# Moving the lower splits of the down chunks from VectorE to GpSimd

## The chip, the cores and the metric

The kernel runs on one core of one Trainium2 chip. The metric is the device time of one execution in microseconds (us). Before the change the median of three runs is 1020.29 us (1019.63 to 1021.06). For this kernel about 0.2% (2 us) is what a measurement can tell from no change.

## The reference

The reference is two transformer-like blocks over 256 tokens of width 1024, in float32. The first block mixes a gated spatial branch and a gated causal convolution and ends in a feed-forward of width 4096. The second block has two layers: differential attention and a gated feed-forward, then latent attention (called here the second attention) and a second gated feed-forward. The change touches these parts:

```python
def conv_ffn(h, w_up, conv_w, conv_b, w_down):      # FFN_HIDDEN = 2816, both layers
    u = h @ w_up                                    # 256 x 1024 @ 1024 x 5632
    c = causal depthwise convolution of width 3 over u, + conv_b
    g, val = jnp.split(c, 2, axis=-1)
    return (jax.nn.silu(g) * val) @ w_down          # 256 x 2816 @ 2816 x 1024

def mla_attention(h, w_in, ..., w_uq, w_ukv, w_o, cos, sin):
    proj = h @ w_in
    q = (rms_norm(proj[..., :384]) @ w_uq) ...      # 16 heads of 64 + 32
    kv = (rms_norm(proj[..., 384:640]) @ w_ukv) ...
    ... masked softmax per head ...
    return o @ w_o
```

Each layer adds the result to x and normalises x before the next.

## The kernel before

**Precision by splitting.** Every weight matrix is read once, in chunks. A chunk lands in SBUF as float32 in one of the raw slots (`raw`, or `q_sb` where that buffer is free), 128 partitions by up to 2048 words. ScalarE copies it, rounded, into the upper half of a ring slot (`whl[..., 0, ...]`, L1267): the upper split. VectorE then writes raw minus upper into the lower half (`whl[..., 1, ...]`, L1763): the lower split. TensorE multiplies upper by upper, upper by lower and lower by upper (L623 to L625, L630 to L632, L825 and L827). So each chunk passes DMA, ScalarE, VectorE and TensorE, in the order of its number n. `hi_ready` and `lo_ready` count the upper and lower splits, `chunk_used` the chunks that TensorE has finished. The ring has four slots: ScalarE may split chunk n once TensorE has used n - 4. The DMA queue (SyncE) loads into a raw slot once the lower split of the chunk that was in it is counted.

**A gated feed-forward** has 22 units (`FB`), one for each 128 hidden columns of the gate and of the value. Unit j has an up chunk (128 x 2048 words, the two halves of `w_up`) and a down chunk (128 x 1024 words, one block of rows of `w_down`). TensorE's order is up j+3, down j+1, and so on, in turn: it runs two ups ahead of the downs. The chunks are numbered in that order within the stage (`n0 + m`): m = 0, 1, 2, 4, 6, ..., 38, 39 are up chunks, m = 3, 5, 7, ..., 37, 40, 41, 42, 43 are down chunks (`is_down`). The last up (39) stands ahead of the last four downs.

Unit j on VectorE, in program order (function `unit` within `ffn`): take the up sum out of PSUM and scale it by the reciprocal deviation (`conv_in`); lower split of the next down chunk, `split(0)`; four convolution taps (L2043, `conv_out`); the product of silu(gate) and value (`t_dve`, L2054); lower split of an up chunk, `split(1)`; and the rest of the rounded product (`lat`, L2058). ScalarE in the same unit: the convolution's first tap with the bias (L1439, after `conv_in`), an upper split of an up chunk, silu (L1444), the rounded product (L1452), an upper split of a down chunk. In the first gated feed-forward the sum is read and scaled in one instruction (L2032, PSUM times `rstd`). In the second (`WIDE`) TensorE makes two sums, ScalarE copies the second (L1431, `t_act`), VectorE adds them (L2028) and scales in place (L2030, `conv_in` times `rstd`).

**At the ends.** Behind the last unit of the first gated feed-forward VectorE splits the first two chunks of the second attention (N_MLA, N_MLA + 1), and only then adds the sums into xT (L2090) and makes the tiles hT (L1838) that TensorE waits for. In the second attention, eight steps of two heads each, VectorE also splits the chunks of `w_uq` (768 words) and of `w_o` (N_WO2 and the three behind it, 2048 words each).

**GpSimd** only copies the rotated key to 16 heads (L1745), once. The program's order on each engine is written out by hand; nothing is scheduled.

## Time and profile before

| | |
|---|---|
| median of three runs | 1020.29 us |
| the profiled execution's own time | 1021.66 us |
| its span, first to last instruction | 1019.8 us |
| TensorE busy | 1003.1 us (98%) |
| VectorE busy | 760.3 us (75%) |
| ScalarE busy | 573.4 us (56%) |
| GpSimd busy | 6.6 us (1%) |
| mean granted TensorE clock | 0.999 of full speed |

Rows of the trace name an engine (PE is TensorE, DVE VectorE, ACT ScalarE, POOL GpSimd), a line of the kernel, out<-in by the program's names, and the partitions by elements. In brackets stands how long the engine had been idle before the row, and what it had waited for. The stages lie thus in the span: differential attention from 427 us, first gated feed-forward from about 536 to 722 us, second attention to 826 us, second gated feed-forward from 826 us to the end.

### The profile page before, as it was taken

How to read it: one execution, taken by the hardware profiler on the slowest of the kernel's cores; microseconds unless marked ns; L12 is line 12 of the kernel's file. 1: busy time of each engine (PE TensorE's matmuls, PEld its weight loads, DVE VectorE, ACT ScalarE, POOL GpSimd, SP SyncE). 2: the span in 40 equal slices, each digit the busy share in tenths (PEclk: the TensorE clock that was granted, in tenths of full speed). 3: DMA queues.
4: the chain of work that ended last, by engine and by line, in shares of the span. 5: the costliest groups of instructions: out<-in, count | busy, mean ns of one | idle time of the engine just before them, and what ended most of it. 6: DMA issues, size and time to landing. Idle time of an engine off the chain costs nothing.

```text
span 1019.8 us, 18671 instructions
## 1 busy us (share of the span) xinstructions
PE 1003.1 (98%) x7220; PEld 932.5 (91%) x7220; DVE 760.3 (75%) x1017; ACT 573.4 (56%) x820; POOL 6.6 (1%) x20
## 2 busy tenths in 40 slices
PE   7999999999999999999999999999999999999997
PEld 6999999999999999977899999999998898888886
DVE  7576655557766656787778877778877888888886
ACT  6543454445544445657866555555646675666665
POOL 0000000000000000000000000000020000000000
PEclk9999999999999999999999999999999999999999
DMA  8645566556665564354464666674324574766651
GB/s 300 211 147 184 184 204 199 171 165 200 199 206 180 191 205 181 128 204 128 167 198 124 189 185 185 186 211 143 125 63 104 166 223 136 216 191 192 191 158 76
DMA packets 191265, 178.87 MB, mean 175 GB/s; under 512 B 17444, under 2 KB 169586, under 8 KB 191218
## 3 DMA queue, kind: packets, MB, share of 16 engines
q1 hardware_dynamic: 191074, 177.96, 56.5%
q8 instruction: 32, 0.52, 0.2%
q10 hardware_dynamic: 144, 0.26, 0.1%
q14 instruction: 15, 0.12, 0.0%
HBM read 177.15 MB, written 1.05 MB: 175 GB/s over the span
## 4 chain that ended last, share of the span: by engine, by line
PE 88%; DVE 5%; ACT 3%; DMA 2%; issue 1%; SPq 0%; DVEq 0%; ACTq 0%
PE psum L623 17%; PE psum L625 17%; PE psum L624 17%; PE psum L825 13%; PE psum L827 7%; PE psum L630 4%; PE psum L632 4%; PE psum L631 4%; DVE whl L1763 2%; ACT whl L1267 1%; DMA raw<-da_w_qkv 1%; DMA raw<-mla_w_o 1%; PE psum L973 1%; PE psum L957 1%; DMA x_rows<-x 1%
## 5 line engine op out<-in xcount | busy, mean ns | idle before, releaser
L1763 DVE TENSOR_TENSOR whl<-raw,whl 128x2048 fp32r<-128x2048 f32 (+2 forms) x145 | 298.2, 2061 | 79.0 <-ACT whl L1267 78.4
L1267 ACT ACTIVATE whl<-raw 128x2048 fp32r<-128x2048 f32 (+2 forms) x145 | 248.3, 1716 | 77.5 <-DMA raw<-w_ff 29.1
L623 PE MATMUL psum<-hT,whl 128*128 128x256 f32 (+1 forms) x784 | 219.9, 280 | 1.0 <-DVE hT L1838 1.0
L624 PE MATMUL psum<-hT,whl 128*128 128x256 f32 (+1 forms) x784 | 218.9, 279 | 0.0
L625 PE MATMUL psum<-hT,whl 128*128 128x256 f32 (+1 forms) x784 | 218.9, 279 | 0.0
L825 PE MATMUL psum<-hT,whl 128*128 128x512 f32 x608 | 213.0, 391 | 0.1
L827 PE MATMUL psum<-hT,whl 128*128 128x256 f32 x608 | 171.4, 282 | 0.0
L623 PEld LDWEIGHTS psum<-hT,whl 128*128 128x128 f32 (+1 forms) x784 | 147.1, 188 | 1.5 <-issue 0.7
L624 PEld LDWEIGHTS psum<-hT,whl 128*128 128x128 f32 (+1 forms) x784 | 147.2, 188 | 0.1
L625 PEld LDWEIGHTS psum<-hT,whl 128*128 128x128 f32 (+1 forms) x784 | 147.1, 188 | 0.0
L623 PE MATMUL psum<-lat,whl 128*128 128x256 f32 (+1 forms) x512 | 144.1, 281 | 0.3 <-DVE whl L1763 0.3
L624 PE MATMUL psum<-lat,whl 128*128 128x256 f32 (+1 forms) x512 | 142.9, 279 | 0.0
L625 PE MATMUL psum<-lat,whl 128*128 128x256 f32 (+1 forms) x512 | 142.9, 279 | 0.0
L825 PEld LDWEIGHTS psum<-hT,whl 128*128 128x128 f32 x608 | 114.1, 188 | 24.4 <-DVE whl L1763 0.5
L827 PEld LDWEIGHTS psum<-hT,whl 128*128 128x128 f32 x608 | 114.9, 189 | 0.8
L1439 ACT ACTIVATE conv_out<-conv_in,vcol 128x256 f32<-128x256 f32 x88 | 48.2, 595 | 92.7 <-DVE conv_in L2032 55.8
L623 PEld LDWEIGHTS psum<-lat,whl 128*128 128x128 f32 (+1 forms) x512 | 95.4, 186 | 2.6 <-issue 1.1
L624 PEld LDWEIGHTS psum<-lat,whl 128*128 128x128 f32 (+1 forms) x512 | 95.4, 186 | 0.1
L625 PEld LDWEIGHTS psum<-lat,whl 128*128 128x128 f32 (+1 forms) x512 | 95.4, 186 | 0.0
L2043 DVE SCALAR_TENSOR_TENSOR conv_out<-conv_in,vcol,conv_out 128x256 f32<-128x256 f32 x176 | 73.6, 479 | 8.8 <-ACT conv_out L1439 8.1
L1763 DVE TENSOR_TENSOR whl<-q_sb,whl 128x2048 fp32r<-128x2048 f32 (+1 forms) x44 | 77.0, 1750 | 0.5 <-ACT whl L1267 0.5
L1267 ACT ACTIVATE whl<-q_sb 128x2048 fp32r<-128x2048 f32 (+1 forms) x44 | 64.9, 1475 | 1.1 <-PE psum L625 1.1
(258 smaller groups left out, 1583.0 us busy)
## 6 DMA issues: line engine op xcount, KB each, us to landing
raw<-w_ff SPq DMA_DIRECT2D x32, 1024.0 KB, 5.6
raw<-w_in SPq DMA_DIRECT2D x24, 1024.0 KB, 5.1
raw<-ffn_w_up SPq DMA_DIRECT2D x44, 512.0 KB, 5.1
q_sb<-ffn_w_up SPq DMA_DIRECT2D x44, 512.0 KB, 5.1
raw<-da_w_qkv SPq DMA_DIRECT2D x12, 1024.0 KB, 5.2
q_sb<-ffn_w_down SPq DMA_DIRECT2D x22, 512.0 KB, 3.8
raw<-ffn_w_down SPq DMA_DIRECT2D x22, 512.0 KB, 3.8
raw<-w_proj_a SPq DMA_DIRECT2D x4, 1024.0 KB, 5.2
```

The lines of the kernel that those rows point to most:

```text
L623: mm(dst, weight(n, 0, cols, kt, c0, m), hi, start=start, stop=False, skip_group_check=True)
L624: mm(dst, weight(n, 0, cols, kt, c0, m), lo, start=False, stop=False, skip_group_check=True)
L625: return mm(dst, weight(n, 1, cols, kt, c0, m), hi, start=False, stop=stop, skip_group_check=True)
L630: mm(dst, hi, w_hi, start=start, stop=False, skip_group_check=True)
L631: mm(dst, hi, w_lo, start=False, stop=False, skip_group_check=True)
L632: return mm(dst, lo, w_hi, start=False, stop=stop, skip_group_check=True)
L825: mm(up_sums[q][:, b], weight(n, 0, PAIR, kt, b * P, P), hT[:, kt], start=kt == 0, stop=False, skip_group_check=True)
L827: last = mm(up_sums[q][:, b, 0, :], weight(n, 1, PAIR, kt, b * P, P), hT[:, kt, 0, :], start=False, stop=kt == KT - 1, skip_group_check=True)
L1267: fn(whl[:, slot, 0, 0:w], landing(n)[:, 0:w], ACT.Copy).then_inc(hi_ready, 1)
L1439: ins = fn(conv_out[:, q, b, :], conv_in[:, q, b, 2:], ACT.Identity, bias=conv(3, b, j), scale=conv(2, b, j))
L1763: tt(whl[:, slot, 1, 0:w], landing(n)[:, 0:w], whl[:, slot, 0, 0:w].bitcast(F32), ALU.subtract).then_inc(lo_ready, 1)
L2043: return stt(dst, conv_in[:, q, b, t:SEQ + t], vcol[:, bass.ds(j + (conv_col(l - 1, t) + FB * b), 1)], dst, ALU.mult, ALU.add)
```

## The change

A lower split on GpSimd waits for its upper split and for the lower split of the chunk before it, so that `lo_ready` still counts in order; a lower split on VectorE that follows one on GpSimd waits for that. Four things change:

- GpSimd does the lower splits of all 44 down chunks of the two gated feed-forwards (128 x 1024 each).
- It does those of N_MLA + 1, N_WO2 and N_WO2 + 1 (128 x 2048 each).
- VectorE's split of the chunk N_UQ + 3 stands ahead of its second query step instead of behind it.
- On ScalarE, in the differential attention, the first `take_columns` stands ahead of an upper split instead of behind it.

```diff
@@ @block.scalar, differential attention
             take_rows(0, 1)
+            take_columns(0, 0)
             split_hi(n + 2)
-            take_columns(0, 0)
             take_columns(0, 1)
@@ @block.gpsimd
+            def split_lo(n, i=0):
+                pool.wait_ge(hi_ready, i * RING + (n + 1))
+                pool.wait_ge(lo_ready, i * RING + n)
+                w = chunk_words(n)
+                nc.gpsimd.tensor_tensor(whl[:, n % RING, 1, 0:w], landing(n)[:, 0:w], whl[:, n % RING, 0, 0:w].bitcast(F32),
+                                        ALU.subtract).then_inc(lo_ready, 1)
+
+            def down_splits(n0):
+                split_lo(n0 + 3)
+                split_lo(n0 + 5)
+                with pool.Fori(0, FB // 2 - 3) as i:
+                    split_lo(n0 + 7, i)
+                    split_lo(n0 + 9, i)
+                for m in range(2 * FB - 4, 2 * FB):
+                    split_lo(n0 + m)
+
+            down_splits(N_FFN0)
+            split_lo(N_MLA + 1)
             pool.wait_ge(kpe_ready, 1)
...
             ins.then_inc(kpe_spread, 1)
+            split_lo(N_WO2)
+            split_lo(N_WO2 + 1)
+            down_splits(N_FFN1)
@@ @block.vector, ffn, unit
                     def split(k):
-                        if k < len(ahead):
+                        if k < len(ahead) and not (l > 0 and is_down(ahead[k] + (i * RING if isinstance(i, int) else 0))):
+                            if l > 0:
+                                dve.wait_ge(lo_ready, i * RING + (n0 + ahead[k]))
                             split_lo(n0 + ahead[k], i)
@@ behind the last unit
                     unit(units - 1, 2 * units - 5, ahead=(2 * units - 1,))
-                    split_lo(n0 + 2 * units)
-                    split_lo(n0 + 2 * units + 1)
+                    if l == 1:
+                        dve.wait_ge(lo_ready, N_MLA)
+                        split_lo(N_MLA)
@@ second attention
+            dve.wait_ge(lo_ready, N_MLA + 2)
             split_lo(N_MLA + LEAD)
...
                 if c == 1:
                     next_query(1)
+                    split_lo(N_UQ + 1 + LEAD)
...
-                if c < 8:
+                if 1 < c < 6:
                     split_lo(N_UQ + c + LEAD)
             normalise_pair(7)
+            dve.wait_ge(lo_ready, N_WO2 + 2)
             split_lo(N_WO2 + LEAD)
```

VectorE in the loop over the units of the second gated feed-forward, before, from the split of an up chunk at the end of one unit to the taps of the next:

```order
L1763 TENSOR_TENSOR whl<-raw,whl 128x2048 [waits hi_ready]
L2058 TENSOR_TENSOR lat<-t_dve,lat 128x256 [waits z_hi2]
L1767 REGISTER_ALU
L2027 REGISTER_ALU [waits chunk_used]
L2028 TENSOR_TENSOR conv_in<-psum,t_act 128x2x256 [waits low2]
L2030 TENSOR_TENSOR conv_in<-conv_in,rstd 128x2x256 [waits up_read2]
L1762 REGISTER_ALU
L1763 TENSOR_TENSOR whl<-raw,whl 128x1024 [waits hi_ready]
L2043 ISA [waits conv_b2]
L2043 SCALAR_TENSOR_TENSOR conv_out<-conv_in,vcol,conv_out 128x256
L2043 ISA
L2043 SCALAR_TENSOR_TENSOR conv_out<-conv_in,vcol,conv_out 128x256
```

And after the change, over the same stretch:

```order
L1786 REGISTER_ALU [waits lo_ready]
L1787 TENSOR_TENSOR whl<-raw,whl 128x2048 [waits hi_ready]
L2086 TENSOR_TENSOR lat<-t_dve,lat 128x256 [waits z_hi2]
L1791 REGISTER_ALU
L2055 REGISTER_ALU [waits chunk_used]
L2056 TENSOR_TENSOR conv_in<-psum,t_act 128x2x256 [waits low2]
L2058 TENSOR_TENSOR conv_in<-conv_in,rstd 128x2x256 [waits up_read2]
L2071 ISA [waits conv_b2]
L2071 SCALAR_TENSOR_TENSOR conv_out<-conv_in,vcol,conv_out 128x256
L2071 ISA
L2071 SCALAR_TENSOR_TENSOR conv_out<-conv_in,vcol,conv_out 128x256
```

The split of 1024 words between the scaling (L2030, now L2058) and the taps is gone from VectorE; the split of 2048 words has a wait for `lo_ready` ahead of it. The removed instruction stands now in GpSimd's order. Its part for the second attention and the second gated feed-forward is this (L1748 is a lower split; behind these rows stand the splits of the last four down chunks):

```order
L1748 TENSOR_TENSOR whl<-raw,whl 128x2048 [waits lo_ready,hi_ready] x2
L1748 TENSOR_TENSOR whl<-q_sb,whl 128x1024 [waits lo_ready,hi_ready]
L1748 TENSOR_TENSOR whl<-raw,whl 128x1024 [waits lo_ready,hi_ready]
L1755 UNCONDITIONAL_BRANCH
L1755 ISA
L1746 REGISTER_ALU [waits hi_ready]
L1748 TENSOR_TENSOR whl<-q_sb,whl 128x1024 [waits lo_ready]
L1745 REGISTER_ALU
L1746 REGISTER_ALU [waits hi_ready]
L1748 TENSOR_TENSOR whl<-raw,whl 128x1024 [waits lo_ready]
L1755 REGISTER_ALU
L1755 COMPARE_AND_BRANCH
```

Before, the copies of the key, which precede these rows now, were all that GpSimd did. On ScalarE, in the differential attention, before:

```order
L1267 ACTIVATE whl<-raw 128x2048
L1569 ACTIVATE k_sb<-psum,r_da 128x512 x2
L1267 ACTIVATE whl<-raw 128x2048
L1576 ACTIVATE q_sb<-psum 128x4x128 x2
L1267 ACTIVATE whl<-raw 128x2048
L1569 ACTIVATE k_sb<-psum,r_da 128x512 x2
```

And after the change:

```order
L1569 ACTIVATE k_sb<-psum,r_da 128x512 x2
L1576 ACTIVATE q_sb<-psum 128x4x128
L1267 ACTIVATE whl<-raw 128x2048
L1576 ACTIVATE q_sb<-psum 128x4x128
L1267 ACTIVATE whl<-raw 128x2048
L1569 ACTIVATE k_sb<-psum,r_da 128x512 x2
```

The first of the two reads of turned columns (L1576) has moved ahead of one upper split.

## Rows read from the trace of the kernel before

**Rows 1.** The page: busy us of each engine, share of the span, instructions.

```profile
PE 1003.1 (98%) x7220; PEld 932.5 (91%) x7220; DVE 760.3 (75%) x1017; ACT 573.4 (56%) x820; POOL 6.6 (1%) x20
```

**Rows 2.** PE's waits: who waited for whom, us in total, times, longest.

```profile
PE psum L623 <- DVE hT L1838: 1.0, 2, 0.6
...
PE psum L947 <- ACT q_sb L1576: 0.7, 1, 0.7
...
PE psum L623 <- DVE whl L1763: 0.6, 2, 0.3
```

**Rows 3.** Windows: busy us (x instructions) by engine; clock, DMA share, GB/s.

```profile
856.00:1000.00 144.00, 143.91 (x762) 123.30 (x761) 125.07 (x177) 89.72 (x123) 0.00 (x0) 1.00 0.63 186
```

**Rows 4.** PE's timeline, second gated feed-forward: first matmuls of ups 4 and 20.

```profile
856.68 0.51 PE L825 MATMUL psum<-hT,whl 128*128 128x512 f32 x1
...
990.54 0.40 PE L825 MATMUL psum<-hT,whl 128*128 128x512 f32 x1
```

**Rows 5.** DVE's timeline, second gated feed-forward, early: start, us, line, [idle before].

```profile
862.11 2.28 DVE L1763 TENSOR_TENSOR whl<-raw,whl 128x2048 fp32r<-128x2048 f32 x1
864.31 0.41 DVE L2058 TENSOR_TENSOR lat<-t_dve,lat 128x256 fp32r<-128x256 f32 x1
864.65 0.68 DVE L2028 TENSOR_TENSOR conv_in<-psum,t_act 128x512 f32<-128x512 f32 x1
865.36 0.69 DVE L2030 TENSOR_TENSOR conv_in<-conv_in,rstd 128x512 f32<-128x512 f32 x1
865.97 1.22 DVE L1763 TENSOR_TENSOR whl<-raw,whl 128x1024 fp32r<-128x1024 f32 x1
867.48 1.67 DVE L2043 SCALAR_TENSOR_TENSOR conv_out<-conv_in,vcol,conv_out 128x256 f32<-128x256 f32 x4 [0.29 <-ACT conv_out L1439]
...
873.15 0.69 DVE L2030 TENSOR_TENSOR conv_in<-conv_in,rstd 128x512 f32<-128x512 f32 x1
```

**Rows 6.** DVE's timeline, second gated feed-forward, late.

```profile
904.98 0.69 DVE L2028 TENSOR_TENSOR conv_in<-psum,t_act 128x512 f32<-128x512 f32 x1 [0.49 <-ACT t_act L1431]
...
1009.15 0.42 DVE L2058 TENSOR_TENSOR lat<-t_dve,lat 128x256 fp32r<-128x256 f32 x1 [0.48 <-ACT lat L1452]
```

**Rows 7.** POOL's timeline at the key's copies: all 16, and the first alone.

```profile
748.80 6.38 POOL L1745 COPY k_sb<-hf 64x256 f32<-64x256 f32 x16 [748.35 <-DVE hf L2300]
...
748.80 1.18 POOL L1745 COPY k_sb<-hf 64x256 f32<-64x256 f32 x1 [748.35 <-DVE hf L2300]
```

**Rows 8.** DVE's timeline beside these copies.

```profile
748.76 0.96 DVE L1763 TENSOR_TENSOR whl<-raw,whl 128x768 fp32r<-128x768 f32 x1
749.75 2.48 DVE L2317 TENSOR_TENSOR k_sb<-psum,rstd 64x512 f32<-64x512 f32 x4
752.72 3.26 DVE L1763 TENSOR_TENSOR whl<-raw,whl 128x768 fp32r<-128x768 f32 x1 [0.50 <-ACT whl L1267]
```

**Rows 9.** DVE's timeline, second gated feed-forward, units 1 and 2.

```profile
843.73 2.29 DVE L1763 TENSOR_TENSOR whl<-raw,whl 128x2048 fp32r<-128x2048 f32 x1
845.93 1.67 DVE L2043 SCALAR_TENSOR_TENSOR conv_out<-conv_in,vcol,conv_out 128x256 f32<-128x256 f32 x4
...
854.34 2.28 DVE L1763 TENSOR_TENSOR whl<-q_sb,whl 128x2048 fp32r<-128x2048 f32 x1
```

**Rows 10.** DVE's timeline, first gated feed-forward.

```profile
612.56 0.69 DVE L2032 TENSOR_TENSOR conv_in<-psum,rstd 128x512 f32<-128x512 f32 x1 [1.25 <-PE psum L625]
...
614.66 1.67 DVE L2043 SCALAR_TENSOR_TENSOR conv_out<-conv_in,vcol,conv_out 128x256 f32<-128x256 f32 x4 [0.28 <-ACT conv_out L1439]
```

**Rows 11.** DVE's and PE's timeline, end of the first gated feed-forward.

```profile
718.17 2.29 DVE L1763 TENSOR_TENSOR whl<-raw,whl 128x2048 fp32r<-128x2048 f32 x1 [0.33 <-ACT whl L1267]
...
722.27 0.35 PE L623 MATMUL psum<-hT,whl 128*128 128x256 f32 x1 [0.55 <-DVE hT L1838]
```

**Rows 12.** ACT's timeline, differential attention.

```profile
436.86 1.92 ACT L1267 ACTIVATE whl<-raw 128x2048 fp32r<-128x2048 f32 x1 [3.43 <-DMA raw<-da_w_qkv]
438.68 0.57 ACT L1576 ACTIVATE q_sb<-psum 128x512 f32<-128x512 f32 x1
```

## The prediction

> **What bounds the kernel now.** I read the page first, then who TensorE waits for, then windows over the stages, then the timelines of the two gated feed-forwards. TensorE is busy 98% of the span [rows 1]. Busy is not full speed, so the second view matters more: behind the first 10 us TensorE waits for another engine less than 3 us in total, and the waits that this change touches are 1.0 us for hT at the end of the first gated feed-forward, 0.7 us for the turned columns and 0.6 us for lower splits in the second attention [rows 2]. In the second gated feed-forward it does not wait (143.91 of 144 us busy, clock 1.00) [rows 3]. Its cadence there: up 4 begins at 856.68 and up 20 at 990.54, 16 units in 133.86 us, so 8.37 us a unit [rows 4]. In such a stage work taken off VectorE gives nothing back. The reader is to see that the most that can be gained is the 2.3 us of waits, and to ask next how near VectorE is to becoming the bound.
>
> It is near. Early in that stage VectorE is behind TensorE and runs without waiting for it, so its rows show its own shortest unit: the scaling L2030 begins at 865.36 and again at 873.15, 7.79 us [rows 5]. It has 0.58 us a unit in hand. Later it has caught up and waits 0.49 us a unit for a sum to be ready [rows 6].
>
> **The removed instruction.** The down split, 1.22 us as a row and 1.14 us to the next start, lies between the scaling and the taps [rows 5]. The taps behind it still waited 0.29 us for ScalarE's first tap (L1439), which itself starts from the scaling. So in the second gated feed-forward the split lies under ScalarE's work: without it the taps start when they did, and the unit stays 7.79 us. The same in the first: there the taps waited 0.28 us too, and the unit as a whole waits 1.25 us for TensorE [rows 10]. Gain per unit: 0.
>
> **What GpSimd's split does to VectorE.** The trace has one place where the two work side by side, the key's copies. GpSimd's copies run from 748.80 to 755.18 [rows 7]. VectorE's split of 768 words takes 0.96 us when it starts ahead of them and 3.26 us when it starts among them at 752.72; it ends at 755.98, 0.80 us behind the last copy, as if it had begun there [rows 8]. It made almost no progress in 2.4 us. The other direction shows too: GpSimd's first copy took 1.18 us, until the split at 748.76 was over, and the other 15 took (6.38 - 1.18) / 15 = 0.35 us each [rows 7]. But VectorE's reads of one PSUM and one SBUF operand ran among the copies at full speed, 2.48 us for four [rows 8]. I read this as: a VectorE instruction with two SBUF operands and a GpSimd instruction that reads SBUF exclude each other. The Trainium skill ("SBUF — State Buffer", section "SBUF: two separate sides") calls this an exclusive lock on a shared port, which whoever starts first holds for its whole instruction; the trace agrees (3.26 us against 0.96), and this rule speaks against the change, since by it the work is moved to an engine that stops the one it relieves.
>
> **How long one takes.** The trace has no two-operand instruction on GpSimd. From below: VectorE's own 1.14 us [rows 5]. By the copy: 1024 words are four times 256, 1.4 us with one operand, and 2.8 us with two if all of the 0.35 us grows with the words [rows 7]. If some 0.1 us of it is fixed (VectorE's splits cost 2.20 us start to start for 2048 words and 1.14 for 1024 [rows 5], so nearly nothing is), two operands take 0.1 + 8 x 0.25 = 2.1 us. The operation reads two operands, so I take 2.3 us, between 2.1 and 2.8, and keep 1.1 and 2.8 as ends. For 2048 words: 4.5 us. The Trainium skill ("GPSIMD Engine Reference", section "3.1 Elementwise — side-by-side cycle accounting") gives 4497 ns for a two-input add of 2048 fp32; half of that, an estimate, is 2.25 us, and by it the sum would be 1 us less. No row here shows it.
>
> **Where it falls in the second gated feed-forward.** GpSimd's split of a down chunk waits for the lower split of the up chunk before it. Its own upper split is done by then. So it is released each time at the end of VectorE's 2048-word split (864.31 in [rows 5]). VectorE goes on at once with L2058 (two SBUF operands, to 864.7), and GpSimd starts behind it, at about +0.40 us. L2028 reads PSUM and runs. L2030 has two SBUF operands; it began at +1.05 us, and now has to wait until 0.40 + 2.3 = 2.70 us. That is 1.65 us on the chain scaling, first tap, upper split, silu, product, 2048-word split, which nothing covers: behind the blocked scaling stand all of these, and TensorE waits for that split. The unit becomes 7.79 + 1.65 = 9.44 us, over TensorE's 8.37 by 1.07 us. Over the 16 units from up 4 to up 20: +17.1 us. With 2.8 us: +25. With 1.4: 8.54 us a unit, +2.7. Below 1.23 us nothing.
>
> At the stage's start there is no reserve to eat first: the split of up 4 ended at 856.54 and TensorE began on it at 856.68 [rows 4, 9]. In unit 1 GpSimd's split is released at 845.93, together with the taps [rows 9]; it goes between them or ahead of the product, and costs 2.1 us either way. At the end units 19 to 21 and four GpSimd splits lie ahead of the last down chunk, for which TensorE has 2 x 5.6 + 3 x 2.8 = 19.6 us (an up has two thirds of the columns of a unit, so of its 8.37 us); three units of some 7 us with two or three blocks of 1 to 2 us make 23 to 25. The last VectorE step ahead of that chunk ends at 1009.57 today [rows 6]. I take +4 us. Sum for the stage: 2.1 + 17.1 + 4 = +23.2 us.
>
> **First gated feed-forward.** GpSimd is released at the same point, but the sum is read and scaled in one instruction with a PSUM operand, which is not held up, and then VectorE has 2.1 us without a two-operand instruction (612.56 to 614.66) behind the 1.25 us of waiting [rows 10]. A GpSimd split of 2.3 us fits. Cost per unit 0. At its start unit 1 is blocked for 2.1 us as in the second stage, and no row shows how much of that TensorE's reserve takes: 0 to 2.1, and as it never waited there I take +0.6. At its end the 2048-word split at 718.17 leaves VectorE [rows 11]; were that all, the 1.0 us of waits for hT would go. But its upper split is done only at 718.1, GpSimd needs it until 722.6, and the tiles hT (two SBUF operands) cannot be made meanwhile; TensorE starts on them at 722.27 today, having waited 0.55 us [rows 11]. With the first tile 0.5 us behind the lock's end that is +0.9 at best, and +3.5 if the four splits before it push the last unit back. I take +2.
>
> **Second attention and differential attention.** N_WO2 on GpSimd takes 4.5 instead of 2.2 us. It need not wait for VectorE's turn, which gives back part of it: between 0 and +2.3 for TensorE's first use, and I take +0.5, since TensorE waited at most 0.3 us for a split there [rows 2]. The earlier split of N_UQ + 3 takes 0.4 of the 0.6 us of waits for splits [rows 2]. The other is read late enough. Together about +0.1. In the differential attention ScalarE waited 3.43 us for a transfer with the turned columns ready, then split for 1.8 us, and only then read them [rows 12]; read first, they cost nothing, since the split still starts when its data land: -0.7 [rows 2].
>
> **Sum.** 23.2 + 0.6 + 2 + 0.1 - 0.7 = +25.2 us, on the profiled execution's 1021.66 us (span 1019.8 and 1.9 around it): 1046.9. The median of the runs lies 1.4 us lower: 1045.5 us.
>
> **The rivals.**
> 1. *The same lock, a shorter instruction* (1.4 to 2.0 us). The stage's start costs 1.2 to 1.8, the 16 units 3 to 12, the end 1 to 3, the rest 1: 1026 to 1038 us, say 1032. For it: the copy's 0.35 us may hold a large fixed part. Against: the operation has two operands.
> 2. *Faster: the lock does not hold for this instruction, or is passed on in small turns.* Then GpSimd's splits lie beside everything, the three waits of [rows 2] shrink by some 2 us, and the time is 1018.3 us. It decides by one thing: whether L2030 keeps its 0.69 us beside a GpSimd split. For it: the copies were a train of sixteen, this is one instruction per unit with 6 us of pause. Against: in that train VectorE did not get one turn in 2.4 us.
> 3. *GpSimd gets in ahead of L2058.* Then L2058 waits too, the block is 2.3 us, not 1.65, the unit 10.1 us: +27 over the 16 units, 1058 us. For it: nothing reserves the order. Against: L2058 is ready and follows the split without a gap [rows 5].
> 4. *No difference that can be told*: an instruction of under 1.2 us or a block that the reserve of 0.58 us covers; small losses and gains cancel at 1020.5 us.
>
> **How the numbers follow.** My forecast has 0.60 (1038 to 1054), rival 1 0.15, rival 2 0.12, rival 3 0.08, rival 4 0.05. About 0.2% (2 us) is what a measurement of this kernel tells from no change. Slower by more: 0.60 + 0.15 + 0.08 = 0.83. Within: 0.05. Faster: 0.12. The range goes from 1021 us, which leaves out rival 2 and half of rival 4, to 1058, which leaves out half of rival 3: 0.18 outside.
>
> **What would show it.** In the changed profile: GpSimd's split of 1024 words with 2.1 to 2.8 us; L2058, the scaling of the second gated feed-forward there, at 2.3 us instead of 0.69 from its start, or starting late; units of 9.4 us in that stage, with TensorE waiting about 1 us in each for a 2048-word split; the first gated feed-forward's units still 8.4 us; the wait for L1576 gone. The prediction is wrong if the scaling keeps its 0.69 us beside GpSimd's split, or if VectorE still waits for TensorE's sums in the second gated feed-forward.

## The result and the profile after

The changed kernel takes 1058.96 us (median of four runs, 1056.47 to 1060.86) against 1020.25 us before: a ratio of 1.0377, 95% interval 1.035 to 1.0405. It is slower by 38.7 us where +25.2 us was forecast, and 1 us above the range given. The profiled execution took 1057.36 us, with a span of 1055.5 us: 35.7 us more than the span before.

The page of the changed kernel, busy us by engine, answers to [rows 1]:

```profile
PE 1013.8 (96%) x7220; PEld 937.2 (89%) x7220; DVE 753.6 (71%) x970; ACT 572.1 (54%) x820; POOL 130.4 (12%) x67
```

47 instructions have left VectorE, by their rows in the kernel before (1.14 and 2.20 us each, start to start) some 57 us of work, and it is busy only 6.7 us less: while one of its instructions stands still, it is counted as busy, and most of the time came back in that form. TensorE's waits now, answering to [rows 2] (us in total, times, longest):

```profile
PE psum L825 <- DVE whl L1787: 11.1, 15, 2.2
PE psum L957 <- DVE prob L2367: 6.6, 3, 3.9
PE psum L630 <- DVE lat L2086: 5.7, 2, 3.2
...
PE psum L623 <- DVE hT L1862: 3.3, 1, 3.3
```

The four shown are waits for VectorE. TensorE's timeline dates them. These are its rows at the marks used below: a down chunk late in the first gated feed-forward (697.17), its wait for hT at that stage's end, the first product behind the norm's sum (733.57), the two long waits for `prob` in the second attention, the first up of the second gated feed-forward (836.85), its ups 4 and 20 (869.26, 1017.22) and the two waits at the end.

```profile
697.17 0.28 PE L623 MATMUL psum<-lat,whl 128*128 128x256 f32 x1
...
726.08 0.36 PE L623 MATMUL psum<-hT,whl 128*128 128x256 f32 x1 [3.34 <-DVE hT L1862]
...
733.57 0.47 PE L623 MATMUL psum<-hT,whl 128*128 128x256 f32 x1
...
801.14 0.88 PE L957 MATMUL psum<-const,prob 128*128 128x128 f32 x6 [3.86 <-DVE prob L2367]
...
810.23 0.87 PE L957 MATMUL psum<-const,prob 128*128 128x128 f32 x6 [2.19 <-DVE prob L2367]
...
836.85 0.39 PE L825 MATMUL psum<-hT,whl 128*128 128x512 f32 x1
...
869.26 0.50 PE L825 MATMUL psum<-hT,whl 128*128 128x512 f32 x1 [2.23 <-DVE whl L1787]
...
1017.22 0.49 PE L825 MATMUL psum<-hT,whl 128*128 128x512 f32 x1 [0.50 <-DVE whl L1787]
...
1036.59 0.47 PE L630 MATMUL psum<-whl,lat 128*128 128x512 f32 x1 [2.41 <-DVE lat L2086]
...
1044.41 0.76 PE L630 MATMUL psum<-whl,lat 128*128 128x512 f32 x1 [3.25 <-DVE lat L2086]
```

The same marks in the kernel before, beside [rows 4]:

```profile
696.36 0.28 PE L623 MATMUL psum<-lat,whl 128*128 128x256 f32 x1
...
729.07 0.47 PE L623 MATMUL psum<-hT,whl 128*128 128x256 f32 x1
...
826.41 0.39 PE L825 MATMUL psum<-hT,whl 128*128 128x512 f32 x1
```

The differences between the two profiled executions, from mark to mark, make this table. The forecast column is the prediction's own sum.

| stretch | forecast, us | measured, us |
|---|---|---|
| to 696.36 before (attention of the first layer, start and loop of the first gated feed-forward) | -0.1 | +0.8 |
| end of the first gated feed-forward, to 729.07 before | +2 | +3.7 |
| second attention, to 826.41 before | +0.1 | +5.9 |
| start of the second gated feed-forward, to up 4 | +2.1 | +2.1 |
| 16 units, up 4 to up 20 | +17.1 | +14.1 |
| the end, to the end of the span | +4 | +9.0 |
| sum | +25.2 | +35.7 |

The mechanism stands in VectorE's rows of the second gated feed-forward, answering to [rows 5] (L2058 is the scaling now, L2086 the rest of the product):

```profile
924.66 0.42 DVE L2086 TENSOR_TENSOR lat<-t_dve,lat 128x256 fp32r<-128x256 f32 x1
925.00 0.68 DVE L2056 TENSOR_TENSOR conv_in<-psum,t_act 128x512 f32<-128x512 f32 x1
925.72 2.18 DVE L2058 TENSOR_TENSOR conv_in<-conv_in,rstd 128x512 f32<-128x512 f32 x1
929.31 1.67 DVE L2071 SCALAR_TENSOR_TENSOR conv_out<-conv_in,vcol,conv_out 128x256 f32<-128x256 f32 x4 [1.42 <-ACT conv_out L1439]
...
934.98 2.17 DVE L2058 TENSOR_TENSOR conv_in<-conv_in,rstd 128x512 f32<-128x512 f32 x1
```

GpSimd beside it:

```profile
924.83 2.52 POOL L1748 TENSOR_TENSOR whl<-q_sb,whl 128x1024 fp32r<-128x1024 f32 x1 [6.75 <-DVE whl L1787]
```

The scaling takes 2.18 us instead of 0.69: it ends 0.55 us behind GpSimd's subtract (927.35). The instruction between, which reads PSUM, keeps its 0.68 us. The scaling recurs every 9.26 us, and 7.79 + (2.18 - 0.69) = 9.28. TensorE, whose own unit is 8.37 us, follows at that pace and waits for a lower split in nearly each. At the end of the stage VectorE's scalings and taps stand too (before, [rows 5], 0.69 us for a scaling and 1.67 for four taps):

```profile
1021.66 3.42 DVE L2071 SCALAR_TENSOR_TENSOR conv_out<-conv_in,vcol,conv_out 128x256 f32<-128x256 f32 x3
...
1028.38 1.73 DVE L2058 TENSOR_TENSOR conv_in<-conv_in,rstd 128x512 f32<-128x512 f32 x1
1031.27 3.81 DVE L2071 SCALAR_TENSOR_TENSOR conv_out<-conv_in,vcol,conv_out 128x256 f32<-128x256 f32 x4 [1.16 <-ACT conv_out L1439]
...
1038.25 1.69 DVE L2058 TENSOR_TENSOR conv_in<-conv_in,rstd 128x512 f32<-128x512 f32 x1
```

### The profile page after: what moved, and what is told of

Read it like the earlier page. It is cut to its first block, busy times and chain, and to the rows that moved or that the text cites. A ratio compares the mean times of both kernels' runs of the same rounds, so it can differ in the third digit from the quotient of the medians.

```text
span 1055.5 us, 18795 instructions
## 1 busy us (share of the span) xinstructions
PE 1013.8 (96%) x7220; PEld 937.2 (89%) x7220; DVE 753.6 (71%) x970; ACT 572.1 (54%) x820; POOL 130.4 (12%) x67
## 4 chain that ended last, share of the span: by engine, by line
PE 66%; DVE 18%; ACT 8%; issue 4%; DMA 2%; DVEq 0%; ACTq 0%; SPq 0%
PE psum L623 16%; PE psum L625 15%; PE psum L624 15%; PE psum L825 7%; DVE whl L1787 5%; ACT whl L1267 4%; PE psum L827 4%; DVE conv_in L2058 3%; DVE conv_out L2071 2%; PE psum L630 2%; PE psum L632 1%; PE psum L631 1%; DMA raw<-da_w_qkv 1%; ACT conv_out L1439 1%; DVE conv_in L2056 1%
## 5 line engine op out<-in xcount | busy, mean ns | idle before, releaser
L1787 DVE TENSOR_TENSOR whl<-raw,whl 128x2048 fp32r<-128x2048 f32 (+1 forms) x120 | 264.2, 2208 | 80.1 <-ACT whl L1267 79.5
L825 PE MATMUL psum<-hT,whl 128*128 128x512 f32 x608 | 215.8, 396 | 11.1 <-DVE whl L1787 11.1
L1748 POOL TENSOR_TENSOR whl<-q_sb,whl 128x1024 fp32r<-128x1024 f32 x22 | 54.8, 2492 | 693.9 <-ACT whl L1267 587.2
L2071 DVE SCALAR_TENSOR_TENSOR conv_out<-conv_in,vcol,conv_out 128x256 f32<-128x256 f32 x176 | 88.3, 563 | 54.1 <-ACT conv_out L1439 54.1
L1748 POOL TENSOR_TENSOR whl<-raw,whl 128x1024 fp32r<-128x1024 f32 (+1 forms) x25 | 69.0, 2759 | 187.9 <-DVE whl L1787 140.7
```

What stands on the lines that cost most here:

```text
L825: mm(up_sums[q][:, b], weight(n, 0, PAIR, kt, b * P, P), hT[:, kt], start=kt == 0, stop=False, skip_group_check=True)
L1748: nc.gpsimd.tensor_tensor(whl[:, n % RING, 1, 0:w], landing(n)[:, 0:w], whl[:, n % RING, 0, 0:w].bitcast(F32), ALU.subtract).then_inc(lo_r ...
L1787: tt(whl[:, slot, 1, 0:w], landing(n)[:, 0:w], whl[:, slot, 0, 0:w].bitcast(F32), ALU.subtract).then_inc(lo_ready, 1)
L2071: return stt(dst, conv_in[:, q, b, t:SEQ + t], vcol[:, bass.ds(j + (conv_col(l - 1, t) + FB * b), 1)], dst, ALU.mult, ALU.add)
```

## The experiments

Each was timed against the kernel before in the same session (1020.39 to 1020.74 us). Line numbers are each kernel's own, so the same operation has other numbers in each.

### The change in four parts

The two orders alone (r1), the first gated feed-forward's down splits alone (r2), N_MLA + 1, N_WO2 and N_WO2 + 1 alone (r3), the second gated feed-forward's down splits alone (r4). GpSimd's program in them:

```diff
 r2    +            down_splits(N_FFN0)
 r3    +            split_lo(N_MLA + 1)
       ...
 r3    +            split_lo(N_WO2)
 r3    +            split_lo(N_WO2 + 1)
 r4    +            down_splits(N_FFN1)
```

r1: 

> Only the two orders are changed; GpSimd does no split. Both theories: the wait for the turned columns (0.7 us) and that for the split of N_UQ + 3 (0.4 us) go, nothing else moves: 1.1 us faster than before, 1019.1 us.

r2: 

> Only the down chunks of the first gated feed-forward go to GpSimd. Theory of the lock (a GpSimd instruction that reads SBUF stops VectorE's instructions with two SBUF operands): units stay at 8.4 us, +0.7 us at the start of the stage, +1.5 to 2.5 us at its end where four GpSimd splits push the last unit back: +2 to +3 us. Rival (the loss is only that a lower split is ready later, 2.5 us instead of 1.1, and its chunk is waited for): the chunks have some 5 us of reserve there: 0 to +0.3 us.

r3: 

> Only N_MLA + 1, N_WO2 and N_WO2 + 1 go to GpSimd. Theory of the lock: the normalisation L2367 is stopped for about 4 us twice in the second attention (6 to 7 us with the slower TensorE clock behind the waits), the tiles hT at the end of the first gated feed-forward once for 1 to 2 us: +7 to +9 us. Rival (only the later lower split): N_WO2 is ready 2.4 us later, of which 1.3 us are won by the earlier start: +1 to +2 us.

r4: 

> Only the down chunks of the second gated feed-forward go to GpSimd. Theory of the lock: +2.1 us at the start and 1.5 us for the slower clock behind that wait, 16 units of 9.26 instead of 8.37 us (+14), +8 to +9 us at the end: +25 to +28 us, units of 9.26 us. Rival (only the later lower split): the down chunk has 5 us of reserve: 0 to +1 us, units of 8.37 us.

| part | time, us | ratio, 95% interval | over before, us |
|---|---|---|---|
| r1 orders | 1020.19 | 0.9993 (0.9985 to 1.0002) | -0.5 |
| r2 first feed-forward | 1023.68 | 1.0024 (1.0013 to 1.0034) | +3.0 |
| r3 three big splits | 1031.4 | 1.01 (1.0079 to 1.0121) | +10.7 |
| r4 second feed-forward | 1047.32 | 1.0259 (1.0237 to 1.028) | +26.7 |

Their sum is +39.9 us, the whole change +38.7: the parts nearly add. The orders did remove the wait for the turned columns (0.67 us at 439.40 before), but in the same stage, ahead of another product at 462.67, a new wait of 0.74 us came, and no gain can be told:

```profile
PE psum L959 <- DVE attn L2204: 0.7, 1, 0.7
```

r1, r2 and r4 came out at or near what was expected, r1 with half of its 1.1 us and no effect that can be told from zero. r3 came out above the +7 to +9 us expected: three instructions cost 10.7 us (8 to 12 by its interval). Its wait:

```profile
PE psum L959 <- DVE prob L2380: 6.4, 2, 3.9
```

### What in GpSimd's work stops VectorE

The splits stay on VectorE as before. At the same 22 points of the second gated feed-forward GpSimd works on `v_sb`, which nobody needs there: a subtract with two operands (r5), a copy of twice the size with one (r6), a memset with none (r7).

```diff
+            for k, m in enumerate([*range(3, 2 * FB - 5, 2), *range(2 * FB - 4, 2 * FB)]):
+                ...
+                pool.wait_ge(hi_ready, N_FFN1 + m + 1)
+                pool.wait_ge(lo_ready, N_FFN1 + m)
+ r5             nc.gpsimd.tensor_tensor(v_sb[:, 0, :], v_sb[:, 0, :], v_sb[:, 1, :], ALU.subtract).then_inc(beside, 1)
+ r6             nc.gpsimd.tensor_copy(v_sb[:], v_sb[:]).then_inc(beside, 1)
+ r7             nc.gpsimd.memset(v_sb[:], 0.0).then_inc(beside, 1)
```

r5: 

> The kernel before, with VectorE doing all lower splits; GpSimd subtracts 1024 words of v_sb, which nobody needs then, at the 22 points where it would split the down chunks of the second gated feed-forward. Nobody waits for it but the last stage. The values in v_sb are overwritten later. Theory of the lock: the same loss as with the splits themselves, since only its SBUF reads count: units of 9.2 to 9.3 us, the scaling L2058 held to 2.2 us, +24 to +28 us. Rival (the loss comes from what waits for GpSimd's split): nobody waits, +0 to +0.5 us, units of 8.37 us.

r6: 

> The same, with a copy of 2048 words onto themselves (one SBUF operand) in place of the subtraction. Theory of the lock: a reading GpSimd instruction locks whatever its operands are; its length decides. By the key's copies 2048 words take 2.2 to 2.8 us, so units of 9.0 to 9.5 us and +18 to +30 us. Rival: 0.

r7: 

> The same, with a memset of 2048 words, which reads nothing. If only GpSimd's reads collide with VectorE's second operand: units of 8.37 us, within 1 us of before. If its writes collide as well: the scaling is held as long as the memset lasts, and units go over 8.4 us when that is more than 1.2 us.

The timelines of the three, each time VectorE's scaling and GpSimd's instruction; the subtract:

```profile
931.98 2.18 DVE L2072 TENSOR_TENSOR conv_in<-conv_in,rstd 128x512 f32<-128x512 f32 x1
...
931.18 2.43 POOL L1784 TENSOR_TENSOR v_sb<-v_sb 128x1024 f32<-128x1024 f32 x1 [6.84 <-DVE whl L1801]
```

The copy:

```profile
928.87 1.66 DVE L2072 TENSOR_TENSOR conv_in<-conv_in,rstd 128x512 f32<-128x512 f32 x1
...
928.06 1.94 POOL L1784 COPY v_sb<-v_sb 128x2048 f32<-128x2048 f32 x1 [6.81 <-DVE whl L1801]
```

The memset:

```profile
930.10 0.69 DVE L2072 TENSOR_TENSOR conv_in<-conv_in,rstd 128x512 f32<-128x512 f32 x1
...
928.70 1.81 POOL L1784 MEMSET v_sb<- 128x2048 f32 x1 [6.55 <-DVE whl L1801]
```

| | time, us | ratio, 95% interval | scaling, us | 7.79 + held | unit, us |
|---|---|---|---|---|---|
| r5 subtract | 1045.52 | 1.0246 (1.0229 to 1.0263) | 2.18 | 9.28 | 9.26 |
| r6 copy | 1035.07 | 1.0139 (1.0123 to 1.0156) | 1.66 | 8.76 | 8.75 |
| r7 memset | 1020.57 | 0.9997 (0.9987 to 1.0007) | 0.69 | 7.79 | 8.36 (TensorE's) |

r5 costs nearly what r4 does (+24.9 us against +26.7), though nobody waits for its result and VectorE still has all its splits. So the loss is not a late split, and not anything that follows from the order of `lo_ready`; it is what GpSimd's reading does to an instruction beside it. The memset of r7 was still under way when the scaling began (928.70 + 1.81 = 930.51 against 930.10) and did nothing to it. r6 holds in kind and missed in size: a copy of 2048 words took 1.94 us, not 2.2 to 2.8, so the unit is 8.75 us, not 9.0 to 9.5, and the loss 14.5 us, not 18 to 30. The Trainium skill ("SBUF — State Buffer", section "SBUF: two separate sides") gives a VectorE instruction with two SBUF inputs an exclusive lock only against a GpSimd operation that reads SBUF; the three rows agree, the memset's 0.69 us included.

### Half a split, and a later one

r8 gives GpSimd only the first 512 words of each of these down splits and leaves VectorE the rest, which waits for GpSimd's half (that wait is left out below). r9 is r4 with GpSimd's subtract released behind the scaling of its unit, except for the last four down chunks.

```diff
 r8: GpSimd
-                w = chunk_words(n)
+                w = 512
 r8: VectorE
+                            rest = slice(512, D)
+                            tt(whl[:, n % RING, 1, rest], landing(n)[:, rest], whl[:, n % RING, 0, rest].bitcast(F32),
+                               ALU.subtract).then_inc(lo_ready, 1)
 r9: GpSimd
+                m = n - N_FFN1
+                if 3 < m < 2 * FB - 5:
+                    pool.wait_ge(ffs[2]["scaled"], i * 2 + (m + 1) // 2)
```

r8: 

> Only the second gated feed-forward's down chunks, and of each only the first 512 words on GpSimd; VectorE does the other 512 where it did the whole split, and counts the chunk. Theory of the lock: the GpSimd part takes 1.3 us from 0.4 us behind the 2048-word split, the scaling may start at 1.7 instead of 1.05 us, the unit is 8.4 us, as long as TensorE's: about 0 over the 16 units, +0.8 us at the start, +1 to +3 us at the end: +2 to +4 us in place of the +27 of the whole splits. Rival (any GpSimd work in the chain costs the same, by the hand-over and not by its length): +20 us or more.

r9: 

> Only the down chunks of FFN1 are split on GpSimd, and from chunk 5 on the split also waits for the scaling L2030 of its own unit; so it starts behind the scaling instead of beside it. Theory (a two-operand GpSimd instruction and a VectorE instruction take turns: the one that comes second stands until the other ends): the scaling keeps its 0.69 us, and the split of 2.5 us now meets the four taps of the unit instead, of which the first would start about 1.5 us behind the scaling and is held about 1 us; what the unit loses is about 0.4 to 0.6 us instead of 0.88. With start and end as in the run where only this FFN's splits moved (26.7 us in all, 14 of them in the units) that is about 9 + 1 + 8 = 17 to 20 us over before, a time of 1038 to 1041 us, units of 8.8 to 8.9 us. Rival (what costs is that VectorE does 2.5 us less often in step, wherever the split falls; or the split starts as the hi half comes and is late by what it is delayed): units of 9.26 us or more and 1047 us or more.

r8's timeline:

```profile
931.19 1.07 DVE L2081 TENSOR_TENSOR conv_in<-conv_in,rstd 128x512 f32<-128x512 f32 x1
...
930.30 1.41 POOL L1754 TENSOR_TENSOR whl<-raw,whl 128x512 fp32r<-128x512 f32 x1 [6.75 <-DVE whl L1797]
```

r9's timeline:

```profile
926.88 0.69 DVE L2069 TENSOR_TENSOR conv_in<-conv_in,rstd 128x512 f32<-128x512 f32 x1
928.99 2.71 DVE L2082 SCALAR_TENSOR_TENSOR conv_out<-conv_in,vcol,conv_out 128x256 f32<-128x256 f32 x4 [1.42 <-ACT conv_out L1441]
...
927.82 2.41 POOL L1755 TENSOR_TENSOR whl<-q_sb,whl 128x1024 fp32r<-128x1024 f32 x1 [6.17 <-DVE conv_in L2069]
```

r8 took 1022.63 us, ratio 1.0024 (1.0014 to 1.0034). A GpSimd instruction of 1.41 us holds the scaling for 0.38 us; the scaling recurs after 8.16 us (939.35 - 931.19), 7.79 + 0.38, under TensorE's 8.37. So the steady units cost nothing (up 20 comes 0.15 us later than before), and what is lost lies behind them. Note that even here VectorE's unit has become longer, not shorter, by giving up half a split.

r9 took 1034.93 us, ratio 1.0137 (1.012 to 1.0154), where 1038 to 1041 us was expected: the direction was right and the size off. The scaling keeps its 0.69 us and the taps pay, 2.71 us for four instead of 1.67, held 1.04. The unit is 8.57 us, not the 8.8 to 8.9 expected, because 0.24 of the 1.04 us falls on slack: the product behind the taps used to wait 0.40 us for silu, and here 0.16. The 16 units lose 3.5 us instead of 14. But the waits for `lat` at the end are 7.2 us in total, more than r4's 5.6, so there nothing is saved: the last four splits do not have the new wait.

### Short instructions

r10 is r3, and r12 the whole change, with each split of GpSimd cut into instructions of 512 words back to back:

```diff
-                w = chunk_words(n)
-                nc.gpsimd.tensor_tensor(whl[:, n % RING, 1, 0:w], ..., ALU.subtract).then_inc(lo_ready, 1)
+                for q in range(chunk_words(n) // 512):
+                    part = slice(q * 512, (q + 1) * 512)
+                    ins = nc.gpsimd.tensor_tensor(whl[:, n % RING, 1, part], ..., ALU.subtract)
+                ins.then_inc(lo_ready, 1)
```

r10: 

> The three splits of the second attention and its neighbourhood (N_MLA+1, N_WO2, N_WO2+1) on GpSimd as before in the run of these three alone (1031.4 us, +10.7), but each 2048-word subtract is four instructions of 512 words back to back. Theory A (the lock is handed over as each GpSimd instruction ends, so a VectorE instruction stands for one quarter, about 1.4 us by the 512-word split seen, at most two): L2367 takes about 2 us instead of 4 to 5.4, TensorE's waits for prob shrink from 6.4 to about 1 us, the time is 1023 to 1027 us. Theory B (a train of GpSimd instructions keeps what it has, as the sixteen key copies did with the tap beside them in before): L2367 is held for the whole train, now 4 x 1.4 = 5.6 us instead of 4.6, and the time is 1031 to 1035 us.

r12: 

> The whole change, with each GpSimd split in instructions of 512 words back to back (two for a down chunk, four for a 2048-word chunk); the last one tells lo_ready. Theory (the lock is handed over at the end of each GpSimd instruction, as in the run with quarters of the three big splits, 1023.2 us, and a VectorE instruction beside a 512-word piece stands at 1.07 us instead of 2.2): units of 8.37 us as in before and not 9.25, FFN1's start and end cost about 1 and 2 to 5 us instead of 2.1 and 8.9, FFN0's end about 1 instead of 3, the attention about 1.5 instead of 6.7; no stretch of TensorE at half clock behind a wait in the attention. In all 1024 to 1031 us instead of 1058.96. Rival (a second piece starts at once behind the first and keeps VectorE out, so a split costs what it cost whole): units of 9.2 us or more and 1050 us or more.

The normalisation of the second attention in the changed kernel, VectorE and then GpSimd:

```profile
795.72 5.36 DVE L2367 TENSOR_TENSOR prob<-prob,stat 128x256 f32<-128x256 f32 x2
...
806.15 4.03 DVE L2367 TENSOR_TENSOR prob<-prob,stat 128x256 f32<-128x256 f32 x2
...
795.73 4.80 POOL L1748 TENSOR_TENSOR whl<-raw,whl 128x2048 fp32r<-128x2048 f32 x1 [36.73 <-ACT whl L1267]
...
804.74 4.56 POOL L1748 TENSOR_TENSOR whl<-raw,whl 128x2048 fp32r<-128x2048 f32 x1 [4.21 <-ACT whl L1267]
```

The same in the kernel before:

```profile
803.56 1.03 DVE L2336 TENSOR_TENSOR prob<-prob,stat 128x256 f32<-128x256 f32 x2
```

And in r10:

```profile
798.02 2.16 DVE L2382 TENSOR_TENSOR prob<-prob,stat 128x256 f32<-128x256 f32 x2
...
798.34 5.43 POOL L1754 TENSOR_TENSOR whl<-raw,whl 128x512 fp32r<-128x512 f32 x4 [0.53 <-ACT whl L1269]
```

1.03 us for the pair before, 5.36 and 4.03 beside a whole 2048-word split, 2.16 beside four quarters. GpSimd needs longer in all (5.43 us against 4.56), yet VectorE gets its turn after one quarter. r10 took 1023.2 us, ratio 1.0026 (1.0016 to 1.0035): 8.2 of r3's 10.7 us are gone with nothing changed but the length of GpSimd's instructions. In both runs the first instruction of the pair had begun ahead of GpSimd and ran free; the second took 5.01 us in r3 and 1.82 in r10, where the first quarter ended at 799.63. That refutes the theory of the train, which gave 1031 to 1035 us.

r12 took 1031.29 us, ratio 1.0104 (1.0087 to 1.0121), 0.3 us above the 1024 to 1031 us expected: 27.7 of the whole change's 38.7 us are gone. VectorE and GpSimd in a steady unit, and the taps at the end:

```profile
929.10 1.07 DVE L2060 TENSOR_TENSOR conv_in<-conv_in,rstd 128x512 f32<-128x512 f32 x1
...
1007.45 2.72 DVE L2073 SCALAR_TENSOR_TENSOR conv_out<-conv_in,vcol,conv_out 128x256 f32<-128x256 f32 x4 [1.17 <-ACT conv_out L1439]
...
928.20 3.12 POOL L1749 TENSOR_TENSOR whl<-q_sb,whl 128x512 fp32r<-128x512 f32 x2 [5.04 <-DVE whl L1789]
```

Up 4 to up 20 takes 133.85 us, as in [rows 4]: the term of 14 us is zero. What stays is 4.2 us up to the first up of this stage (830.57 against 826.41), 2.1 at its start, where the expectation said 1, and 3.3 at its end.

### The clock behind a wait

r11 is r3, with TensorE computing 18 matmuls of N_WO2 a second time, with the same values, in the step ahead of a wait for `prob`:

```diff
                 if c == 7:
                     part(N_WO2, range(0, 3))
+                    b = bank[bank_of(N_WO2)]
+                    for kt in range(3):
+                        for blk in range(2):
+                            columns(b[:, blk, :], N_WO2, PAIR, kt, blk * P, P, hi_lo(mT, kt), kt == 0 and blk == 0, False)
```

r11: 

> The same three splits on GpSimd, whole, and TensorE computes 18 matmuls of the output product N_WO2 a second time, with the same values, just ahead of its 3.9 us wait for prob; they take about 2.1 us of the wait. Theory (each long wait of TensorE costs, beyond itself, about 1.7 us, since the matmuls behind it run at a granted clock near 0.5 for a few us): the wait left is about 1.8 us, no stretch near 0.5 follows it around 803 us, and the time falls by about 1.7 us against 1031.4 us, to 1029.7 (+9.0 over before instead of +10.7). Rival (the low stretch belongs to the place, or costs nothing that is not given back): 1031.4 us, +10.7.

Windows of r3 behind its second wait, and then of r11 over the same work (behind the us and the busy times of PE, PEld, DVE, ACT and POOL stand the granted clock, the DMA share and GB/s):

```profile
809.00:810.00 1.00, 1.00 (x6) 0.89 (x5) 0.00 (x0) 1.00 (x2) 0.00 (x0) 0.56 1.06 355
810.00:811.00 1.00, 1.00 (x5) 0.35 (x4) 0.00 (x0) 1.00 (x1) 0.00 (x0) 0.50 1.09 388
811.00:812.00 1.00, 1.00 (x7) 0.62 (x8) 0.83 (x3) 0.48 (x1) 0.00 (x0) 0.50 0.38 130
812.00:813.00 1.00, 1.00 (x10) 0.67 (x7) 0.97 (x4) 0.46 (x2) 0.00 (x0) 0.74 0.00 0
```

```profile
809.00:810.00 1.00, 1.00 (x10) 0.65 (x10) 0.73 (x3) 1.00 (x1) 0.00 (x0) 1.00 1.10 390
```

I had the place wrong: the matmuls fell into the second wait, 2.53 us long in r3, and not into the one of 3.86 us, which is unchanged. There they filled the wait. In r3 TensorE runs at the lower of its two levels (clock 0.50, 1.2 GHz) for some 3 us behind the wait and loses 0.44 + 0.50 + 0.50 + 0.26 = 1.7 us; in r11 the clock stays at 1.00. The first up of the next stage comes 2.6 us earlier (833.55 against 836.15), of which 0.7 us was there at the end of the first long wait (797.79 against 798.50). r11 took 1029.34 us, ratio 1.0086 (1.0069 to 1.0103), against r3's 1031.4. The intervals of the two overlap, so the 2.1 us rest on the trace more than on the times. Useless work in a wait made the kernel no slower, and probably faster by about the 1.7 us. That the filler is what kept the clock up is not shown: at the same place the changed kernel waits 2.19 us without a filler, and its clock stayed at 1.00 too.

The changed kernel has five such stretches, behind its waits of 3.34, 3.86, 2.23, 2.41 and 3.25 us. In each TensorE loses about 1.7 us of its own time. The first two windows lie behind the waits of 3.86 and 3.25 us, the third behind the wait of 2.19 us at 810.23, where the clock stayed at 1.00:

```profile
802.00:804.00 2.00, 2.00 (x9) 1.68 (x7) 0.01 (x1) 1.95 (x2) 0.00 (x0) 0.50 0.99 331
...
1045.00:1047.00 2.00, 2.00 (x6) 1.61 (x5) 0.00 (x0) 0.31 (x2) 0.00 (x0) 0.50 0.00 0
...
810.00:812.00 2.00, 1.77 (x13) 1.72 (x14) 0.51 (x2) 0.86 (x2) 0.00 (x0) 1.00 0.67 229
```

What such a stretch costs the kernel depends on what ends last behind it, and for most of the five it is little:

- Behind 3.34 us (end of the first gated feed-forward): from 726.08 to 733.57 are 7.49 us, against 6.80 for the same work before, which had a wait of 0.41 us in it. It costs 0.7 us.
- Behind 3.86 us (second attention): TensorE's next wait, of 2.19 us, ends with the split that GpSimd began at 804.74 and ended at 809.30. Its upper split had begun at 802.76, with almost nothing of the slow stretch ahead of it. So, as far as these rows tell, the stretch is covered.
- Behind 2.23 us (up 4): the 16 units take 147.96 us, and 16 of VectorE's units of 9.26 make 148.2. It costs nothing.
- Behind 2.41 us: TensorE waits again, 3.25 us, for a product of VectorE's and ScalarE's chain, in which no matmul of the stretch stands. It costs nothing.
- Behind 3.25 us: these are the last 12 matmuls. From the first to the last of them are 4.11 us, against 2.57 before. It costs 1.5 us.

Together that is about 2 us of the 35.7.

Nor does the length of a wait alone say whether the clock falls. It fell behind a wait of 1.77 us in r5, and it stayed at 1.00 behind waits of 2.16 (r12), 2.29 (r2) and 2.43 us (r9), and behind one of 3.06 us in r12, which ended at 1019.49:

```profile
1020.00:1022.00 2.00, 2.00 (x10) 1.60 (x9) 0.00 (x0) 1.23 (x3) 0.00 (x0) 1.00 0.00 0
```

## Why the prediction was right and wrong

**What bounds the kernel, and the removed instruction: right.** VectorE's unit is 9.26 us in r5, which keeps every split on VectorE, and in r4, which takes the down splits off it: the removed instruction was worth nothing there. r8, with half a split taken off and GpSimd's share short, keeps TensorE's 8.37 us and gains nothing. (The prediction puts TensorE's waits behind the first 10 us under 3 us; the rows of the wait view add to 3.7. Nothing in its sum rests on that.)

**The lock: right, and shown.** r5, r6 and r7 separate it from everything else in the change.

**How long one takes: right.** 2.50 us on average for 1024 words (forecast 2.3, 2.1 to 2.8) and 4.64 for 2048 (forecast 4.5).

**The units: right in kind, 3 us too high.** I let GpSimd begin 0.40 us behind the start of L2086 (L2058 before) and take 2.3 us; it began 0.17 us behind it (924.83 against 924.66) and took 2.52. The two errors cancel, by luck: it ended at +2.69 where the forecast has +2.70. What was off is the step behind it: I let the scaling take its full 0.69 us from there, and it ended after 0.55. So it was held 1.49 us, not 1.65, and the unit is 9.26 and not 9.44 us. The rule "7.79 plus what is held" gives the unit of r4, r5, r6, r8 and r12 within 0.02 us. Rival 3, whose 1058 us is nearly the measured time, was wrong: L2086 kept its 0.42 us. Its number does not follow from its own terms either: 27 in place of 17.1 us in the sum gives 1055.4. Rivals 1 and 4 fail by the 2.50 us of a split. Rival 2 fails by the scaling's 2.18 us; turns are passed on, but only between GpSimd's instructions, as r10 and r12 show.

**The start: right,** +2.1 us by the marks, and by the way told: unit 1's taps, beside GpSimd's split, took 3.82 us instead of 1.67. The stretch at half clock behind up 4's wait left nothing in the units' term.

**The first gated feed-forward's loop: right.** Up to 697.17 the changed kernel is 0.8 us late, where -0.1 was forecast together with the orders.

**The second attention: this step failed.** The prediction says: "It need not wait for VectorE's turn, which gives back part of it: between 0 and +2.3 for TensorE's first use, and I take +0.5". It asked only when the split would be ready, not what stands still while it runs. The normalisation `prob` (L2336 before, L2367 now) has two SBUF operands, TensorE waits for it, and the two 4.6 to 4.8 us splits fell squarely on two of the eight. The prediction had worked out the lock further up and applied it to the feed-forwards alone. Measured: +5.9 us for the stretch where +0.1 was forecast, with 6.6 us of waits for `prob` in it; before, TensorE stood 1.3 us in this stretch. r3, with only the three big splits moved, has these waits too (6.4 us), and r10 shows it from the other side.

**The ends: sized too low.** The first feed-forward's end cost 3.7 us, not 2: the pair of hT tiles at 722.13 took 4.20 us, held until GpSimd's split ended at 725.65. The wait is 2.8 us longer than before (3.34 against 0.55), and half clock behind it costs 0.7. The second's cost 9.0, not 4. I had counted "two or three blocks of 1 to 2 us". The four rows of the end show 2.2 us too much in the taps at 1021.66 (three of them, by 1.67 for four 1.25 us when free), 1.0 in each scaling and 2.1 in the taps at 1031.27: 6.3 us in four blocks, because there the splits are released by ScalarE's upper splits and fall on the taps as well. So the last down chunk begins 27.19 us behind up 20 instead of 19.51, 7.7 us more; half clock in its own matmuls, behind the wait of 3.25, adds 1.5, and the steps behind the last matmul are 0.2 shorter.

**The orders: not told.** -0.7 was forecast, r1 shows -0.5 with an interval that holds zero.

**The clock was not in the sum at all.** I priced each new wait at its own length. In the profiled execution the stretches at half clock account for about 2 us, 0.7 and 1.5, both in rows that came out too low. The other 3 us, from 35.7 to 38.7, are spread between executions: the profiled execution lies 1.6 us below the changed kernel's median, and that of before lay 1.4 above its own. The two executions of the changed kernel near 1057 us have a mean granted clock of 0.990, the two near 1061 one of 0.988.

**What stays open.** What decides whether the clock falls behind a wait: its length alone does not. Why VectorE got no turn among the sixteen key copies of [rows 7, 8] but does get one between the quarters of r10. The remaining 11 us of r12 were not taken apart further. None of the kernels run beats the one before.

## What to carry to other kernels

Before moving elementwise work from VectorE to GpSimd, list every VectorE instruction with two SBUF operands that can run beside it, in every stage and not only in the loop, and ask who waits for it: the price is the held time on that chain, and an idle GpSimd says nothing of it. If the work has to go there, cut it into short instructions and release it where no such instruction is due; a cut alone took back 28 of 39 us here. Price a new wait of TensorE at its length, then ask what ends last behind it: the matmuls there can run at half clock, which took 1.7 us of TensorE's time in most cases here, and of that between nothing and all showed in the kernel's time.

## What the runs showed of the hardware

- A VectorE instruction with two SBUF operands that comes while GpSimd subtracts or copies stands until that one GpSimd instruction ends (a scaling of 0.69 us took 2.18 beside a subtract of 2.52); a memset on GpSimd of 1.81 us does not hold it, and an instruction with a PSUM operand keeps its 0.68 us.
- Between two back-to-back GpSimd subtracts VectorE got its turn (not so among the key's copies of [rows 7, 8]): a pair of 1.03 us took 2.16 us beside four quarters, 4.03 to 5.36 beside one whole.
- GpSimd's subtract of two float32 operands over 128 partitions took 1.41 us for 512 words, 2.50 for 1024 and 4.64 for 2048, so about 0.35 us plus 1.07 us for each 512 words. A copy of 2048 words took 1.94 us.
- In the profiled executions TensorE's granted clock fell to 0.50 (1.2 GHz) behind waits of, among others, 1.77 (r5), 2.23, 2.41, 3.25, 3.34 and 3.86 us (changed kernel), 2.53 (r3) and 2.59 us (r4), and stayed at 1.00 behind waits of 2.16 and 3.06 (r12), 2.19 (changed kernel), 2.29 (r2) and 2.43 us (r9), and where a wait was filled with matmuls (r11).
